# Indexer keys, head weights and low rank in one projection; the router's logits in four column groups

## The chip, the cores and the metric

The kernel runs on one core of one Trainium2 chip. The metric is the device time of one launch in microseconds, as the median of several runs.

## The reference

Two decoder layers on 256 tokens of width 1024, all in float32. Each layer has a mixer with four head groups, a cross attention to 256 memory rows, and a feed-forward part: dense SwiGLU in layer 0, and in layer 1 the top 2 of 8 experts. What the change touches:

```python
z = hn @ w_in                        # columns cut into a_q .. a_lr .. c_qi, c_ki, c_wi, d_uv
log_a = log_sigmoid(a_lr @ wa2 + ba) / TAU          # gated linear attention, a_lr: 16 wide
dots  = einsum('bqhd,bsd->bqsh', c_qi, c_ki)        # indexer: 8 heads of 32, one key of 32
score = einsum('bqsh,bqh->bqs', relu(dots), c_wi)   # c_wi: 8 head weights per token
_, sel = top_k(score, 64)                           # 64 keys for each token
...
logits = rmsnorm(h, norm_ffn[1]) @ router           # (256, 8), layer 1 only
top_v, top_i = top_k(logits, 2); gates = softmax(top_v)
```

## The kernel before

The work of each engine is one written-out instruction stream; the engines meet only in semaphores, and nothing is reordered. Activations are kept transposed (`xnT`: features on partitions, 8 tiles of 128 features by 256 tokens). A projection is either `on_features` (weights stationary, 8 matmuls of 256 tokens, result with features on partitions) or `on_tokens` (activations stationary, the weights' columns stream through, result with tokens on partitions). A float32 matmul is two MATMUL instructions in the trace, each with a weight load of its own, so 8 matmuls are `x16` there. A float32 transposition by `pe.transpose` is one.

Weights lie packed in DRAM in units. SyncE loads them in order into a ring of seven slots (`RING`, 4096 floats on each partition), and a slot is loaded anew when TensorE has used it up (`slot_free`). In the mixer the units are: U_QI (indexer queries, keys, head weights), U_A, U_AG (with the low-rank columns), U_CQ, U_CV, U_BU, U_UV.

The mixer of a layer on TensorE begins so: the rows of `h` are turned and normed; queries `qi` (16 matmuls); keys `ki` (8, 32 wide); head weights by `on_tokens` (16 matmuls that stream 8 columns each, L1593); in layer 0 a small bias matmul and three `keep_busy` matmuls (products that nobody reads, L1560), in layer 1 the first half of `a`; then `dots(1)` (L1658). ScalarE copies the keys to four places (L728), scales the head weights (`wis`, L729), later takes the relu of the dots (L741). VectorE then runs `score_and_take(1)` and `(0)`: the weighted sum over heads and 8 rounds of max and replace (L1092 to L1102), and behind them it copies the low rank `lr` (L1067). In layer 0, TensorE also turns the memory rows between the dots and `a` (L1574, memT). After `a`, `av` and `dots(0)` come `lr` (8 matmuls, 16 wide), `ag`, the first half of `q`, the matmul `logit` that needs VectorE's copy of `lr` (L1713), the rest of `q`, `k`, `cv`, and then `att` (L1729), which waits for results of ScalarE and VectorE that follow from `logit`.

The router in layer 1: TensorE turns the rows of `h` by plain matmuls with the identity (L1990), VectorE and ScalarE scale them into `xnT`, two feature tiles each in turn (L1355, L865), 8 matmuls of 8 columns give the logits (L1997), ScalarE copies them (L868), two transpositions put tokens on partitions, and VectorE chooses the experts (from L1365) and builds the tables of jobs. A first expert job of 64 tokens then starts on nine weight units that are loaded ahead: seven in the ring and two in `extra`. The second of these is loaded when `rlog_ps` is 1. The jobs that follow are 21 units each, 2 MB a unit.

Of the kernel before, what the change touches and what calls it, by code (L numbers as in the profile page):

```python
# [8 lines left out]
P = 128  # L9
# [5 lines left out]
ACT = mybir.ActivationFunctionType  # L15
# [4 lines left out]
KT = D // P  # L20
# [44 lines left out]
def packed_blocks():  # L65

    for layer in range(DEPTH):
        for s, (lo, hi) in enumerate(IN_UNITS):
            yield ("in_units", layer, s), "w_in", layer, (0, D), (lo, hi)
        yield ("wkv", layer), "xa_wkv", layer, (0, D), (0, 2 * GW)  # L70
        for i, m in enumerate(WOUT_ORDER):
            yield ("wout", layer, i), "w_out", layer, (256 * m, 256 * m + 256), (0, D)
        yield ("wq", layer), "xa_wq", layer, (0, D), (0, GW)
        yield ("wo", layer), "xa_wo", layer, (0, GW), (0, D)
    for c, n in enumerate(FFN_TILES):
        f0 = P * sum(FFN_TILES[:c])
        for w, name in enumerate(("ffn_w1", "ffn_w3")):
            yield ("ffn", 3 * c + w), name, 0, (0, D), (f0, f0 + n * P)
        yield ("ffn", 3 * c + 2), "ffn_w2", 0, (f0, f0 + n * P), (0, D)
# [7 lines left out]

def pack_weights(inputs):

    return np.concatenate([rows_on_partitions(inputs[name][index, r0:r1, c0:c1])  # L90
                           for _, name, index, (r0, r1), (c0, c1) in packed_blocks()])
# [79 lines left out]
IN_UNITS = ((C_QI, C_UV), (0, 512), (C_AG, C_BU), (C_CQ, C_CV), (C_CV, C_QI), (C_BU, C_CQ), (C_UV, IN_W))  # L171
# [10 lines left out]
for _key, _, _, (_r0, _r1), (_c0, _c1) in packed_blocks():  # L182
    PACKED[_key] = (_at, _at + (_r1 - _r0) * (_c1 - _c0))
    _at = PACKED[_key][1]
# [4 lines left out]

CONST = {}  # L190
_at = 0
for _name, _w in (("ident", P), ("vis", 256), ("reset", 256), ("bd", 256), ("tril", P), ("inv", 512),
                  ("before", P), ("ones", P), ("iota", P), ("eidx", 8), ("erev", 8), ("limit", 16)):
# [5 lines left out]
def shape_constants():  # L199
# [21 lines left out]
    put("erev", 8 - np.arange(8)[None, :])  # L221
    put("limit", np.concatenate(([SMALL], np.full(N_EXP - 1, SMALL - 1), [SMALL + P], np.full(N_EXP - 1, P)))[None, :])
# [14 lines left out]
def build(nc, A, out):  # L237
    ctx = ExitStack()
    with ctx:
# [76 lines left out]
        wa2 = sb("wa2", [GLA_RANK, P])  # L316
# [44 lines left out]
        def count(layer, no, each, off):  # L361
# [12 lines left out]
        lrT = qidx[0:GLA_RANK, 768:1024]  # L374
# [24 lines left out]
        lgT = wsT[0:N_EXP, 0:2, :].rearrange("p a b -> p (a b)")  # L399
# [20 lines left out]
            sel_ready rank_ps jobs_ready j_now j_s j_a j_tps j_th j_t j_yps j_yv j_ya j_g j_gps j_gtps j_gh j_gl  # L420
# [11 lines left out]
        g_ps = {n: slot_free[ENDS[n][0]] if n in ENDS else sem(f"ps_{n}") for n in GROUPS}  # L432
# [69 lines left out]
        def _(sp):  # L502
# [5 lines left out]
            for layer in range(DEPTH):  # L508
# [24 lines left out]

                for s, (lo, hi) in enumerate(IN_UNITS):
                    unit(0, s, ring[:, s, 0:KT * (hi - lo)], packed("in_units", layer, s))
                    if s == 0:
                        for i, name in enumerate(("gla_norm", "sgu_ln_g", "sgu_ln_b")):
                            sp.dma_start(bc[:, i, :], A[name][lay].broadcast_to([P, GW])).then_inc(S["loaded_par"], 16)
                        sp.dma_start(wa2[:, :], A["gla_wa2"][lay].rearrange("e r c -> (e r) c")).then_inc(S["loaded_par"], 16)
# [135 lines left out]
        def _(act):  # L675
# [20 lines left out]
            for layer in range(DEPTH):  # L696
# [171 lines left out]
            act.activation(lgT, ps[4][0:N_EXP, 0:SEQ], ACT.Copy).then_inc(S["xT_a"], 1)  # L868
# [132 lines left out]
        def _(dve):  # L1001
# [37 lines left out]
            for layer in range(DEPTH):  # L1039
# [36 lines left out]
                out_of("qi", qiT, v3(ps[4], 0, 512, 2))  # L1076
                if layer < 1:
# [3 lines left out]
                dve.wait_ge(g_ev["ki"], L1)  # L1081

# [25 lines left out]
                out_of("lr", lrT, ps[4][0:GLA_RANK, 0:256])  # L1108
# [445 lines left out]
        def _(pe):  # L1554
# [65 lines left out]
            for layer in range(DEPTH):  # L1620
# [5 lines left out]
                def w_in(u):  # L1626
                    lo, hi = IN_UNITS[u]
# [612 lines left out]
```

## Time and profile before

| | |
|---|---|
| median of 3 runs | 1389.37 us (1389.14 to 1391.38) |
| the profiled execution: time, span | 1391.46 us, 1389.7 us |
| busy PE, VectorE, ScalarE, GpSimd | 93%, 35%, 27%, 6% of the span |
| the chain that ended last | PE 62%, DMA 32%, VectorE 4%, ScalarE 1%, issue 1% |
| DMA | 433.51 MB, mean 312 GB/s; 424 to 430 GB/s in most slices of the experts' stage |

Layer 0 fills about 0 to 384 us of the span, layer 1 up to the router 384 to 557, router and choice 557 to 576, the experts' jobs 576 to 1380. The chain is followed back from the last instruction, so a piece of time that stands in it would shorten the span if it went, until the next thing comes last. PE rows give the operands' names, partitions times stationary columns, and the shape that streams.

### The profile page before, as it was taken

The page shows a single profiled execution, that of the slowest core. Times are in us where ns is not written, and L with a number is a line of the kernel's source. Part 1 is how long each engine was busy: PE and PEld are TensorE (multiplying, and loading weights), DVE is VectorE, ACT ScalarE, POOL GpSimd, SP SyncE. Part 2 cuts the span into 40 slices and gives each one's busy share as a digit, 9 for nine tenths or more (in the row PEclk, how much of TensorE's full clock was granted, in tenths as well). Part 3 has the DMA queues.
Part 4 walks back from the last instruction along what each step waited for, and adds up shares of the span by engine and source line. Part 5 has one row for each costly group of instructions (what it writes and reads, how often), then busy time and mean ns, then how long its engine had stood idle before and what let it go on. Part 6 is the DMA issues. An engine that isn't in the chain of part 4 may idle for free.

```text
span 1389.7 us, 15762 instructions
## 1 busy us (share of the span) xinstructions
PE 1286.5 (93%) x6338; PEld 785.7 (57%) x6338; DVE 484.4 (35%) x819; ACT 373.7 (27%) x574; POOL 79.9 (6%) x68
## 2 busy tenths in 40 slices
PE   7999999999999999999989879779779778999996
PEld 5777888888888688634323224224224225788532
DVE  1627267777626453600101001001001004988102
ACT  2244154444323423301101001001001005776102
POOL 0263000000004600000000000000000000000000
PEclk9999999999999999999999999999999999999998
DMA  9431633443181308799999999999999999999895
GB/s 361 177 116 37 231 133 137 177 186 137 40 352 65 117 1 365 306 417 428 427 428 426 429 428 430 428 428 427 430 429 428 429 427 430 427 428 379 365 428 244
DMA packets 37416, 433.51 MB, mean 312 GB/s; under 512 B 5726, under 2 KB 7924, under 8 KB 9588
## 3 DMA queue, kind: packets, MB, share of 16 engines
q1 hardware_dynamic: 37172, 432.25, 75.4%
q8 instruction: 37, 0.61, 0.2%
q0 software_dynamic: 192, 0.53, 0.1%
q14 instruction: 15, 0.12, 0.0%
HBM read 431.71 MB, written 1.05 MB: 311 GB/s over the span
## 4 chain that ended last, share of the span: by engine, by line
PE 62%; DMA 32%; DVE 4%; ACT 1%; issue 1%; SPq 0%; DVEq 0%; ACTq 0%
DMA ring<-in_experts 31%; PE bank L2089 10%; PE bank L2169 9%; PE bank L1588 8%; PE bank L1975 6%; PE bank L1593 5%; PE bank L2099 5%; PE bank L1611 4%; PE bank L1979 3%; PE bank L1574 1%; PE bank L1865 1%; PE bank L1866 1%; PE bank L1872 1%; PE bank L2022 1%; PE bank L2047 1%; PE bank L1560 1%
## 5 line engine op out<-in xcount | busy, mean ns | idle before, releaser
L2089 PE MATMUL bank<-ring,xs 128*64 128x512 f32 x1552 | 352.1, 597 | 41.2 <-DMA ring<-in_experts 41.2
L2089 PEld LDWEIGHTS bank<-ring,xs 128*64 128x64 f32 x1552 | 109.6, 137 | 247.9 <-issue 228.4
L2099 PE MATMUL bank<-ring,s_act 128*64 128x512 f32 x768 | 176.3, 597 | 34.5 <-DMA ring<-in_experts 34.3
L1477 DVE TENSOR_TENSOR s_act<-wsT,bank 128x256 f32<-128x256 f32 x49 | 20.6, 421 | 510.8 <-ACT wsT L903 510.8
L2099 PEld LDWEIGHTS bank<-ring,s_act 128*64 128x64 f32 x768 | 55.6, 137 | 142.8 <-issue 131.4
L1975 PE MATMUL bank<-x_both,wf_hi 128*128 128x512 f32 x336 | 118.9, 396 | 0.0
L903 ACT ACTIVATE wsT<-bank 128x256 f32<-128x256 f32 x49 | 18.8, 383 | 336.3 <-PE bank L2047 336.3
L1588 PE MATMUL bank<-xnT,ring 128*128 128x256 f32 (+2 forms) x448 | 102.5, 388 | 0.6 <-ACT bias L752 0.6
L1501 DVE TENSOR_TENSOR ring_lo<-ring,w_hi 128x2048 fp32r<-128x2048 f32 (+1 forms) x44 | 96.0, 2193 | 20.2 <-ACT w_hi L960 20.2
L838 ACT ACTIVATE wf_hi<-ring 128x1024 fp32r<-128x1024 f32 x66 | 69.8, 1060 | 98.6 <-PE bank L1975 67.5
L1979 PE MATMUL bank<-x_both,wf_lo 128*128 128x256 f32 x336 | 94.1, 280 | 0.0
L1272 DVE TENSOR_TENSOR wf_lo<-ring,wf_hi 128x1024 fp32r<-128x1024 f32 x66 | 80.5, 1223 | 33.4 <-ACT wf_hi L838 33.4
L1588 PEld LDWEIGHTS bank<-xnT,ring 128*128 128x128 f32 (+2 forms) x448 | 80.5, 182 | 18.5 <-issue 2.1
L960 ACT ACTIVATE w_hi<-ring 128x2048 fp32r<-128x2048 f32 (+1 forms) x44 | 80.7, 1839 | 34.6 <-PE bank L2169 29.8
L899 ACT ACTIVATE j_act<-bank 128x512 f32<-128x512 f32 x49 | 29.3, 597 | 191.4 <-PE bank L2089 191.4
L1593 PE MATMUL bank<-ring,xnT 128*128 128x256 f32 (+2 forms) x320 | 78.5, 400 | 0.0
L2169 PE MATMUL bank<-w_hi,xg 128*128 128x512 f32 x224 | 72.8, 402 | 2.6 <-DVE xg L1508 2.6
L1975 PEld LDWEIGHTS bank<-x_both,wf_hi 128*128 128x128 f32 x336 | 63.1, 188 | 14.9
L1593 PEld LDWEIGHTS bank<-ring,xnT 128*128 128x128 f32 x320 | 56.4, 193 | 20.9 <-issue 16.0
L1979 PEld LDWEIGHTS bank<-x_both,wf_lo 128*128 128x128 f32 x336 | 63.5, 189 | 0.9
L2169 PEld LDWEIGHTS bank<-w_hi,xg 128*128 128x128 f32 x224 | 42.9, 192 | 13.7 <-issue 3.5
L2047 PEld LDWEIGHTS bank<-cst,j_act 128*128 128x128 f32 x224 | 24.0, 141 | 40.9 <-issue 40.1
(361 smaller groups left out, 1459.8 us busy)
## 6 DMA issues: line engine op xcount, KB each, us to landing
ring<-in_experts SPq DMA_DIRECT2D x166, 2048.0 KB, 29.2
ring<-in_packed SPq DMA_DIRECT2D x18, 1536.0 KB, 6.9
ring<-in_packed SPq DMA_DIRECT2D x11, 2048.0 KB, 10.2
ring<-in_packed SPq DMA_DIRECT2D x16, 1024.0 KB, 4.9
extra<-in_experts SPq DMA_DIRECT2D x2, 2048.0 KB, 11.8
ring<-in_packed SPq DMA_DIRECT2D x2, 1184.0 KB, 6.1
ring<-in_packed SPq DMA_DIRECT2D x2, 1088.0 KB, 10.9
h<-in_x SPq DMA_DIRECT2D x2, 512.0 KB, 4.0
```

Source lines behind the costliest of these rows:

```text
L838: act.activation(as_piece(w, ffn_hi(i)), weights, ACT.Copy).then_inc(S["hi_ready"], 1)
L960: act.activation(w_hi[:, i % NB, 0:hi - lo], ring[:, slot, lo:hi], ACT.Copy)\
L1272: dve.tensor_tensor(as_piece(w, ffn_lo(i)), weights, as_piece(w, ffn_hi(i)), sub)\
L1501: dve.tensor_tensor(ring_lo[slot][:, lo:hi], ring[:, slot, lo:hi], w_hi[:, i % NB, 0:hi - lo], sub).then_inc(S["lo_ready"], 1)
L1588: i = mm(dst, w[:, k, :], src[:, k, :], start=k == 0, stop=k == KT - 1)
L1593: i = mm(dst, src[:, k, P * t:P * t + P], w[:, k, :], start=k == 0, stop=k == KT - 1)
L1611: ins = mm(dst, x, y, start=opens and n % 3 == 0, stop=closes and n % 3 == 2)
L1975: ins = mm(dst[:, :], wh[:, k, :], x_both[:, k, :], start=k == 0, stop=False, skip_group_check=True)
L1979: ins = mm(dst[:, 0:SEQ], wl[:, k, :], x_both[:, k, 0:SEQ], start=False, stop=k == KT - 1, skip_group_check=True)
L2089: i = mm(ps[d % 2][SMALL * side:SMALL * side + SMALL, :], xs[:, k, :], weights(u)[:, at:at + FC], start=k == 0, stop=k == KT - 1)
L2099: i = mm(ps[6 + half][SMALL * side:SMALL * side + SMALL, :], s_act[:, d % 4, x + side, :], weights(u)[:, at:at + FC], start=d == 0 and x = ...
L2169: ins = mm(dst[:, :], st_, mv, start=opens, stop=closes)
```

## The change

Layout of the weights: U_QI now holds queries, keys, the 16 low-rank columns at column 32 of the key group, 16 columns of zeros, and the 8 head weights at column 64. U_AG loses the low rank. One `on_features` of 72 columns replaces keys (32), head weights and low rank (16), and its rows land on partitions 0, 32 and 64. VectorE copies head weights and low rank out at once, TensorE turns the head weights by two small transpositions behind `dots(1)`, and VectorE scales them into `wis`. `ag` has a new wait for the first scoring, since it overwrites the bank. In the router the rows of `h` are turned by `pe.transpose`; the logits are four partial sums, one for each group of 32 columns of the array, two matmuls each; ScalarE copies 104 rows in place of 8, and a matmul with the constant `parts` adds the four parts and turns them.

```diff
+IN_UNITS = (((C_QI, C_WI), (C_LR, C_BU), (None, AT_WI - AT_LR - GLA_RANK), (C_WI, C_UV)),
+            ((0, 512),), ((C_AG, C_LR),), ((C_CQ, C_CV),), ((C_CV, C_QI),), ((C_BU, C_CQ),), ((C_UV, IN_W),))
...
 ScalarE
                 for q in range(4):
-                    act.activation(kiT[32 * q:32 * q + 32, :], ps[5][0:32, 0:256], ACT.Copy)
-                act.activation(wis[:, :, :], v3(ps[5], 256, 272, 2), ACT.Copy,
-                               scale=float(IDX_HEADS ** -0.5 * IDX_DIM ** -0.5)).then_inc(g_ev["ki"], 1)
+                    i = act.activation(kiT[32 * q:32 * q + 32, :], ps[5][0:32, 0:256], ACT.Copy)
+                i.then_inc(g_ev["ki"], 1)
...
-            act.activation(lgT, ps[4][0:N_EXP, 0:SEQ], ACT.Copy).then_inc(S["xT_a"], 1)
+            act.activation(lgT, ps[4][0:LG_ROWS, 0:SEQ], ACT.Copy).then_inc(S["xT_a"], 1)
...
 VectorE
                 out_of("qi", qiT, v3(ps[4], 0, 512, 2))
+                group("ki")
+                dve.tensor_copy(wiT, ps[5][AT_WI:AT_WI + IDX_HEADS, 0:256])
+                dve.tensor_copy(lrT, ps[5][AT_LR:AT_LR + GLA_RANK, 0:256]).then_inc(g_ev["lr"], 1)
+                dve.wait_ge(S["wi_ps"], L1)
+                link(dve.tensor_scalar(wis[:, :, :], v3(ps[5], 256, 272, 2), float(IDX_HEADS ** -0.5 * IDX_DIM ** -0.5), None,
+                                       mult))
...
-                out_of("lr", lrT, ps[4][0:GLA_RANK, 0:256])
                 group("logit")
...
 TensorE
-                on_features(ps[5][0:32, 0:256], w[:, :, 256:288])
-                for t in range(TT):
-                    i = on_tokens(ps[5][:, 256 + 8 * t:264 + 8 * t], w[:, :, 288:296], t)
-                i.then_inc(g_ps["ki"], 1)
+                on_features(ps[5][0:AT_WI + IDX_HEADS, 0:256], w[:, :, 256:256 + AT_WI + IDX_HEADS]).then_inc(g_ps["ki"], 1)
...
                 dots(1, 256).then_inc(S["dots_ps"], 1)
+                pe.wait_ge(g_ev["lr"], L1)
+                for t in range(TT):
+                    i = pe.transpose(ps[5][:, 256 + IDX_HEADS * t:256 + IDX_HEADS * (t + 1)], wiT[:, P * t:P * t + P],
+                                     ident[AT_WI:AT_WI + IDX_HEADS, AT_WI:AT_WI + IDX_HEADS])
+                i.then_inc(S["wi_ps"], 1)
...
                 pe.wait_ge(arrived[U_AG], landed[0])
+                pe.wait_ge(S["scored"], first)
...
-                on_features(ps[4][0:GLA_RANK, 0:256], w[:, :, 256:272]).then_inc(g_ps["lr"], 1)
...
-                    i = mm(xT(kt)[:, P * t:P * t + P], h[:, t, P * kt:P * kt + P], ident, start=True, stop=True)
+                    i = pe.transpose(xT(kt)[:, P * t:P * t + P], h[:, t, P * kt:P * kt + P], ident)
...
-            for kt in range(KT):
-                if kt % 2 == 0:
-                    b = kt // 2
+            for q in (0, 2):
+                for b in (q, q + 1):
                     normed(1, norm_no(1, 2), b)
-                i = mm(ps[4][0:N_EXP, 0:SEQ], routw[:, kt, :], xnT[:, kt, :], start=kt == 0, stop=kt == KT - 1)
+                for x in range(2):
+                    for b in (q, q + 1):
+                        i = mm(ps[4][QUADRANT * b:QUADRANT * b + N_EXP, 0:SEQ], routw[:, 2 * b + x, :], xnT[:, 2 * b + x, :],
+                               start=x == 0, stop=x == 1, tile_position=(0, QUADRANT * b))
...
-                i = pe.transpose(ps[5][:, N_EXP * t:N_EXP * t + N_EXP], lgT[:, P * t:P * t + P], ident[0:N_EXP, 0:N_EXP])
+                i = mm(ps[5][:, N_EXP * t:N_EXP * t + N_EXP], lgT[:, P * t:P * t + P], cc("parts")[0:LG_ROWS, :],
+                       start=True, stop=True)
```

TensorE, layer 0, from the projection of the queries to the first half of `ag`, before (a matmul is one row here, `bank` is any PSUM bank, `qidx` holds the indexer's queries and keys):

```order
L1588 MATMUL bank<-xnT,ring 32x256 x8
L1593 MATMUL bank<-ring,xnT 128x8 x16
L1649 MATMUL bank<-gla,kdec 4x384
L1560 MATMUL bank<-cst 128x256 x3
L1658 MATMUL bank<-qidx 128x256 x8
L1574 MATMUL bank<-diag,memT 128x128 x16
...
L1658 MATMUL bank<-qidx 128x128 x8
L1588 MATMUL bank<-xnT,ring 16x256 x8
L1593 MATMUL bank<-ring,xnT 128x256 x16
```

The same stretch of the changed kernel, whose lines have other numbers:

```order
L1610 MATMUL bank<-xnT,ring 72x256 x8
L1667 MATMUL bank<-gla,kdec 4x384
L1582 MATMUL bank<-cst 128x256 x3
L1676 MATMUL bank<-qidx 128x256 x8
L1689 MATMUL bank<-cst,qidx 128x8 x2
L1596 MATMUL bank<-diag,memT 128x128 x16
...
L1676 MATMUL bank<-qidx 128x128 x8
L1615 MATMUL bank<-ring,xnT 128x256 x16
```

The 16 matmuls of 8 columns and the 8 of 16 rows are gone, and two transpositions (L1689) stand behind the dots.

VectorE in the same place of the changed kernel (before, `qidx<-bank 128x512` is followed at once by the reciprocals for the memory rows):

```order
L1086 COPY qidx<-bank 128x512
L1097 COPY qidx<-bank 8x256
L1098 COPY qidx<-bank 16x256
L1100 TENSOR_SCALAR wis<-bank 128x16
L1033 RECIPROCAL st<-st 128x1
L1034 TENSOR_SCALAR diag<-cst,st 128x128
```

Two copies and the scaling have come ahead of the factors `diag` that TensorE's transpositions of the memory rows need.

## Rows read from the trace of the kernel before

**Rows 1.** The page: its span, and the granted clock in 40 slices.

```profile
span 1389.7 us, 15762 instructions
...
PEclk9999999999999999999999999999999999999998
```

**Rows 2.** The chain of work that ended last, layer 0: start us, us, what.

```profile
26.85 3.67 PE bank L1593 x32
31.25 2.33 PE bank L1560 x6
33.59 1.86 PE bank L1658 x16
```

**Rows 3.** The same chain, layer 1.

```profile
400.90 4.24 PE bank L1593 x32
405.13 6.34 PE bank L1588 x16
411.47 1.12 PE bank L1658 x16
```

**Rows 4.** Busy time by stretch: each engine, its instructions, granted clock, DMA share, GB/s.

```profile
31.18:35.38 4.20, 4.20 (x23) 2.68 (x23) 0.45 (x2) 4.09 (x11) 0.77 (x1) 0.59 1.02 425
403.80:410.60 6.80, 6.80 (x20) 5.71 (x21) 0.00 (x0) 1.67 (x5) 0.00 (x0) 0.50 0.96 364
```

**Rows 5.** Timeline of layer 0: start us, us, engine, line, operation, idle before.

```profile
34.23 0.29 DVE L1015 TENSOR_SCALAR diag<-cst,st 128x128 f32<-128x128 f32 x1
...
35.38 3.84 PE L1574 MATMUL bank<-diag,memT 128*128 128x128 f32 x32
...
59.53 3.61 PE L1588 MATMUL bank<-xnT,ring 128*16 128x256 f32 x16 [0.61 <-ACT bias L752]
```

**Rows 6.** Timeline of layer 1.

```profile
415.13 0.48 DVE L1092 SCALAR_TENSOR_TENSOR score<-r,wis,cst 128x256 f32<-128x256 f32 x1 [17.08 <-ACT r L741]
...
424.08 3.63 PE L1588 MATMUL bank<-xnT,ring 128*16 128x256 f32 x16
...
438.59 0.67 PE L1713 MATMUL bank<-qidx,wa 16*128 16x256 f32 x2 [0.32 <-DVE qidx L1067]
...
446.25 1.69 ACT L771 ACTIVATE r<-gla 32x256 f32<-32x256 f32 x4 [0.49 <-DVE gla L1115]
...
456.56 1.88 PE L1729 MATMUL bank<-r,gla 128*128 128x512 f32 x4
```

**Rows 7.** Timeline of the router in layer 1.

```profile
556.93 3.73 PE L1990 MATMUL bank<-cst,h 128*128 128x128 f32 x32
...
559.36 1.77 DVE L1355 TENSOR_SCALAR xnT<-bank,pcol 128x256 f32<-128x256 f32 x4 [0.94 <-PE bank L1990]
...
559.83 1.71 ACT L865 ACTIVATE xnT<-bank,pcol 128x256 f32<-128x256 f32 x4
...
560.59 3.62 PE L1997 MATMUL bank<-xnT,routw 128*8 128x256 f32 x16
...
561.43 2.48 DVE L1362 SCALAR_TENSOR_TENSOR r<-h,st,uvg 128x1024 f32<-128x1024 f32 x2
...
565.10 0.49 DVE L1365 TENSOR_SCALAR score<-bank,st 128x8 f32<-128x8 f32 x2 [1.18 <-PE bank L2002]
```

**Rows 8.** Timeline of layer 0, two halves of the array's columns.

```profile
123.96 0.43 PE L1809 MATMUL bank<-zeros,gla 128*64 128x256 f32 x1
...
123.97 0.43 PE L1809 MATMUL bank<-Sst,gla 128*64 128x256 f32 x1
...
124.23 0.38 PE L1809 MATMUL bank<-zeros,gla 128*64 128x256 f32 x1
```

**Rows 9.** Busy time of line L1913 alone: PE, its weight loads, granted clock.

```profile
178.10:180.40 2.30, 2.10 (x16) 1.66 (x16) 1.00 0.48 96
```

**Rows 10.** Timeline: SyncE's issues of expert weights.

```profile
579.86 20.42 SPq L581 DMA_DIRECT2D ring<-in_experts  x6
```

**Rows 11.** The chain again, expert stage.

```profile
683.65 23.70 DMA ring<-in_experts
```

More of the change, by code:

```diff
@@ L67, in packed_blocks @@
     for layer in range(DEPTH):
[L68 to L70 removed]
+        for s, columns in enumerate(IN_UNITS):
+            yield ("in_units", layer, s), "w_in", layer, (0, D), columns
+        yield ("wkv", layer), "xa_wkv", layer, (0, D), ((0, 2 * GW),)
         for i, m in enumerate(WOUT_ORDER):
[L72 to L74 removed]
+            yield ("wout", layer, i), "w_out", layer, (256 * m, 256 * m + 256), ((0, D),)
+        yield ("wq", layer), "xa_wq", layer, (0, D), ((0, GW),)
+        yield ("wo", layer), "xa_wo", layer, (0, GW), ((0, D),)
     for c, n in enumerate(FFN_TILES):
@@ L85, in rows_on_partitions, with columns_of @@
     return np.ascontiguousarray(block.reshape(rows // P, P, cols).swapaxes(0, 1)).reshape(-1)
+def columns_of(rows, columns):
+    return np.concatenate([np.zeros((len(rows), hi), np.float32) if lo is None else rows[:, lo:hi] for lo, hi in columns], axis=1)
 def pack_weights(inputs):
-    return np.concatenate([rows_on_partitions(inputs[name][index, r0:r1, c0:c1])
-                           for _, name, index, (r0, r1), (c0, c1) in packed_blocks()])
+    return np.concatenate([rows_on_partitions(columns_of(inputs[name][index, r0:r1], columns))
+                           for _, name, index, (r0, r1), columns in packed_blocks()])
 def pack_experts(inputs):
@@ L169, with unit_width @@
 C_CQ, C_CK, C_CV, C_QI, C_KI, C_WI, C_UV = 1040, 1296, 1552, 1808, 2064, 2096, 2104
-IN_UNITS = ((C_QI, C_UV), (0, 512), (C_AG, C_BU), (C_CQ, C_CV), (C_CV, C_QI), (C_BU, C_CQ), (C_UV, IN_W))
+QUADRANT = 32
+AT_LR, AT_WI = QUADRANT, 2 * QUADRANT
+IN_UNITS = (((C_QI, C_WI), (C_LR, C_BU), (None, AT_WI - AT_LR - GLA_RANK), (C_WI, C_UV)),
+            ((0, 512),), ((C_AG, C_LR),), ((C_CQ, C_CV),), ((C_CV, C_QI),), ((C_BU, C_CQ),), ((C_UV, IN_W),))
+def unit_width(s):
+    return sum(hi if lo is None else hi - lo for lo, hi in IN_UNITS[s])
 U_QI, U_A, U_AG, U_CQ, U_CV, U_BU, U_UV = range(7)
@@ L181 @@
 PACKED, _at = {}, 0
-for _key, _, _, (_r0, _r1), (_c0, _c1) in packed_blocks():
-    PACKED[_key] = (_at, _at + (_r1 - _r0) * (_c1 - _c0))
+for _key, _, _, (_r0, _r1), _columns in packed_blocks():
+    PACKED[_key] = (_at, _at + (_r1 - _r0) * sum(hi if lo is None else hi - lo for lo, hi in _columns))
     _at = PACKED[_key][1]
 R_MIX, R_XA, R_MEM, R_FFN, R_BA, R_PB, R_PS, R_SB, N_ROWS = 0, 8, 16, 24, 32, 33, 35, 37, 41
+LG_ROWS = 3 * QUADRANT + N_EXP
 CONST = {}
@@ L532, in unit @@
                     sp.dma_start(dst, src).then_inc(arrived[s], 16)
-                for s, (lo, hi) in enumerate(IN_UNITS):
-                    unit(0, s, ring[:, s, 0:KT * (hi - lo)], packed("in_units", layer, s))
+                for s in range(len(IN_UNITS)):
+                    unit(0, s, ring[:, s, 0:KT * unit_width(s)], packed("in_units", layer, s))
                     if s == 0:
```

24 lines of the change are left out of this document (12 added, 12 removed).

## Prediction

> **What bounds the kernel now.** I read the page first: the span, and the granted clock, nine tenths or more in every slice but the last [rows 1]. Then the chain of work that ended last. Up to the experts it is almost all TensorE, piece behind piece, and three of its pieces are what the change is about: 32 instructions of L1593, which stream 8 columns each, take 3.67 us in layer 0 and 4.24 in layer 1 [rows 2, 3]. In the experts' stage the chain turns to DMA at 683.65 [rows 11]. That does not make the time before it free: the weights are loaded into slots that TensorE must give back, and SyncE issues again only at 579.86, when the first job has used its first unit [rows 10]. From there DMA and TensorE lean on one another to the end, so whatever brings the first job forward brings the end forward by as much. The question is thus how much earlier the first job starts.
>
> The last view is the table by stretches, cut where pieces of the chain looked too long. 16 instructions of 128x256 cost 3.6 us elsewhere [rows 5, 6], but the same 16 behind the head weights of layer 1 cost 6.34 [rows 3]. The table says why: from 403.80 to 410.60 the granted clock was 0.50, the lower of the two levels, 1.2 GHz, and from 31.18 to 35.38 it was 0.59 on the mean [rows 4]. Both times TensorE had just spent about 4 us on the narrow products. They cost more than their own time.
>
> **Layer 0.** Gone are the head weights, 3.67 us. The key group has 72 columns in place of 32; what a matmul costs is what streams, 256 columns, and 8 of them with 16 stationary columns took 3.61 us [rows 5], like those with 128, so I cost the widening at nothing. Three `keep_busy` matmuls took 2.33 us and the dots 1.86 at the low clock [rows 2]; at the full clock they are 6 x 3.6/16 = 1.35 and, from layer 1, 1.12 [rows 3], a gain of 1.7. The two small transpositions cost 0.13 each, from 16 transpositions in 2.10 us [rows 9]: 0.26. TensorE would then reach the memory rows at 35.38 - 3.67 - 1.7 + 0.26 = 30.3. But `diag` of those rows comes from ScalarE and VectorE. VectorE made it at 34.23 [rows 5], and that path moves only by the 3.67, to 30.6; ahead of it now stands the scaling of the head weights, which waits for the transpositions (30.3) and takes some 0.2 us. The factor is ready at about 31.0, and the gain so far is 4.3, not 5.1. Queued behind VectorE's new wait are just these factors, and for them TensorE waits: that is the 0.8. Later the low rank goes, another 3.6 [rows 5]. The wait of 0.61 for ScalarE ahead of it stays, since both sides moved alike; it now holds `ag`. **Layer 0: 7.9 us.**
>
> **Layer 1.** Head weights 4.24 less 0.26; the low clock behind them 6.34 - 3.5 = 2.8; the low rank 3.55; and the wait of `logit` for VectorE's copy of the low rank, 0.32 [rows 6], goes too, since the copy now comes before the scoring. Sum 10.65, say **10.7 us**. What is late next? VectorE's scoring was nearly level with TensorE. It starts at 415.13, on the relu of the dots, and that moves by all but the low rank and the wait, 6.8 us. Behind it come the bias of the logits, ScalarE's exponentials, and the block-diagonal queries (L771), which end at 446.25 + 1.69 = 447.94 [rows 6], now 441.1. TensorE asks for them at 456.56, now 445.9. The slack shrinks from 8.6 to 4.8 and holds. The new wait of `ag` for the first scoring asks for eight sums of about 0.5 us from 408.3 on, done at 412.5, when TensorE comes there at 417: free. If that cover went, each us would be paid in full.
>
> The added DMA traffic is 32 columns more in one unit and 16 less in another, of 1024 rows of 4 bytes: 131 KB, 0.3 us at 425 GB/s [rows 4], ahead of units that are in place long before their use. The change moves no issue of SyncE past another, and the slots of the key unit and of `ag` come free earlier. ScalarE loses one small copy. I cost these at nothing.
>
> **The router.** 32 instructions in 3.57 us (556.93 to 560.6) become 16 transpositions, 2.1 us at the rate of [rows 9]. This gives little: VectorE's scaling starts 0.5 earlier, but ScalarE's starts at 559.83, held by its own sums of squares, and ends at 561.54 [rows 7]. The logits now begin when ScalarE has its first pair, about 560.7, and their second half when it has the last, 561.6. What follows depends on whether column groups work side by side. The trace has halves of the array doing so: two matmuls with 64 columns each start at 123.96 and 123.97, the next pass at 124.23 [rows 8], 0.27 for two where one behind the other would be 0.44. At that rate the last four matmuls are four pairs of instructions, 1.1 us, and end at 562.7; before, 16 in a row ended at 564.1. That is 1.4 less. The wider copy and the summing matmul (two passes and full weights in place of one each) give back about 0.1. VectorE must be free as well: its two products (L1362) take 2.48 us and end near 563.4, and the choice would start at 563.8 against 565.10 [rows 7]. **Router: 1.3 us**; none if the groups run one behind the other (8 x 0.22 = 1.8 from 561.6 or the full 3.5 from 560.7 both end near 564), and 1.6 if the groups cost less than the halves. I take 1.3, since the row of the halves is the same kind of packing.
>
> Here a rule of the skill speaks against the change. The router's turning was made of plain matmuls, and 16 transpositions take their place. In this trace 16 such transpositions ran in 2.10 us at a granted clock of 1.00 [rows 9], so I take no loss of clock. The Trainium skill, "TensorE: Matmul & The Clock Gate", Part 4 on PE-mode transpose, says that transpositions do not count as activity for the clock as matmuls do; by that rule the low clock would come in the router. That is the first rival below.
>
> **The sum.** 7.9 + 10.7 + 1.3 = 19.9 us. Against the profiled execution that is 1391.46 - 19.9 = 1371.6. The median of the runs shown is 2.1 lower, 1389.37, and gives 1369.5. Some of the difference may lie in the two low-clock stretches that I price at 4.5 us together, which need not be as long in each execution; so I say 1370.0.
>
> **Rivals.**
> - The clock falls at a new place (0.19). In the router TensorE now transposes, waits about 1 us for ScalarE, does short bursts and waits again. For it: both falls of before followed thin work. Against: it did not fall at 178. Priced by the rows, a stretch at 0.5 costs half its length: 4.2 us at 0.59 cost 1.7, 6.8 us cost 2.8 [rows 4]. In the router it would take away the 1.3 and delay the products of rank or gather by 2 or so: 1373.5. The same happens if it falls when TensorE waits for the memory rows' copies in layer 0.
> - Something hides the gain (0.08). The slack of 4.8 us in layer 1 is my own working, and POOL's scaling and SyncE's loads follow the same scoring. If another chain takes over behind `att` in both layers and only half of the mixers' 18.6 is kept: 1379. Against: the chain shows TensorE nearly without a break up to the router.
> - The column groups do nothing (0.10): the router gives 0, 1371.3. Within the range.
> - Slower than before (0.03): the low clock, once it falls in the router, stays. In the experts' stage TensorE is on the chain alone until 683.65 [rows 11]; each us at 1.2 GHz there costs half. The gain of 20 is used up after 40 us of it, and 60 us would give 1370 + 30 = 1400. Against it: the two stretches of before ended within 7 us, as soon as full matmuls streamed.
> - As forecast: 0.60.
>
> **How the numbers follow.** The likeliest case alone spans 1368 to 1372.5: the router's 0 to 1.6, and 1.5 us either way for how long the low clock lasted in the runs shown. The clock rival adds up to 1376; below, 1366.5 takes in a median that keeps the whole price of the low clock and 1.6 in the router with 2 us of scatter as in the three runs. 1366.5 to 1376 leaves out the hidden gain and the slower case, 0.11, and with the tails of the others 0.18. A measurement of this kernel tells a change from none at about 0.2%, 2.8 us. Faster by more than that: 0.95, all cases but the last and a gain lost nearly whole; within it 0.02; slower 0.03.
>
> **What the profile after would show.** No instructions of 128x8 in the mixers; granted clock 1.00 in both places; the first half of `a` in layer 1 in 3.5 us; `dots(1)` some 6.5 us after the keys; the first scoring at about 408.3 - 7.9 = 400; `att` reached without a wait; 16 logit instructions starting in pairs 0.27 apart, the choice 1.3 us earlier against the turning's start; SyncE's issue of 579.86 at about 560. The prediction is wrong if the clock row is below 1.00 in the router, if TensorE waits ahead of `ag` or `att`, or if SyncE's issue moves by less than 17.

## The result and the profile after

The changed kernel takes 1371.14 us (median of 4 runs, 1370.39 to 1372.91), the kernel before on the same chip 1390.38 us (4 runs, 1389.14 to 1393.55). The ratio is 0.9863, with a 95% interval from 0.9844 to 0.9881: 19.2 us faster, where 20 was forecast (1370.0, range 1366.5 to 1376.0). The profiled execution took 1372.91, with a span of 1369.3.

From the page of the changed kernel, its span and the granted clock in 40 slices:

```profile
span 1369.3 us, 15555 instructions
...
PEclk9999999999999999999999999999999999999998
```

The chain of work that ended last, changed kernel (start us, us, what), which answers to [rows 2, 3, 11]: layer 0, layer 1, experts.

```profile
28.10 1.49 PE bank L1582 x6
29.59 1.08 PE bank L1676 x16
31.62 3.82 PE bank L1596 x32
...
84.42 1.72 PE bank L1752 x4
...
397.04 1.08 PE bank L1676 x16
398.77 3.46 PE bank L1610 x16
...
664.14 23.55 DMA ring<-in_experts
```

`att` of layer 0 in the same chain of the kernel before:

```profile
91.79 1.72 PE bank L1729 x4
```

The narrow matmuls of the head weights have gone. The three `keep_busy` take 1.49 in place of 2.33, the dots 1.08 in place of 1.86, and the first half of `a` in layer 1 takes 3.46 in place of 6.34. The DMA transfer at which the chain turns starts 19.51 us earlier (683.65 to 664.14).

Busy time by stretch, changed kernel, the places of [rows 4] and the router (stretch, length, busy us of PE, its weight loads, VectorE, ScalarE, POOL, then the granted clock, DMA share, GB/s):

```profile
26.50:31.60 5.10, 4.23 (x30) 2.44 (x29) 1.47 (x5) 4.11 (x9) 0.77 (x1) 1.00 1.00 419
31.60:38.70 7.10, 5.57 (x42) 5.20 (x43) 3.58 (x10) 3.69 (x11) 2.13 (x3) 1.00 1.03 431
393.50:398.60 5.10, 5.10 (x39) 4.26 (x38) 1.01 (x3) 1.91 (x5) 0.00 (x0) 1.00 1.04 442
...
542.60:544.40 1.80, 1.72 (x17) 0.70 (x17) 1.77 (x3) 0.67 (x2) 0.00 (x0) 1.00 1.00 419
```

The clock is 1.00 in each of them. Neither low stretch of [rows 4] is left, and none came in the router, behind the 16 transpositions.

The timeline of the changed kernel (start us, us, engine, line, operation, idle time before it and who ended it), at the first projection and at the places of [rows 5 to 7] and [rows 10]:

```profile
16.84 10.53 PE L1610 MATMUL bank<-xnT,ring 128*128 128x256 f32 x48
...
30.77 0.17 DVE L1100 TENSOR_SCALAR wis<-bank 128x16 f32<-128x16 f32 x1 [2.52 <-PE bank L1689]
...
31.18 0.29 DVE L1034 TENSOR_SCALAR diag<-cst,st 128x128 f32<-128x128 f32 x1
...
31.62 3.81 PE L1596 MATMUL bank<-diag,memT 128*128 128x128 f32 x32 [0.89 <-DVE diag L1034]
...
55.73 7.14 PE L1615 MATMUL bank<-ring,xnT 128*128 128x256 f32 x32 [0.61 <-ACT bias L771]
...
400.28 0.48 DVE L1115 SCALAR_TENSOR_TENSOR score<-r,wis,cst 128x256 f32<-128x256 f32 x1 [1.88 <-ACT r L760]
...
404.48 0.06 DVE L1120 MEMSET st<- 128x1 f32 x1
...
409.72 7.17 PE L1615 MATMUL bank<-ring,xnT 128*128 128x256 f32 x32
...
430.10 1.69 ACT L790 ACTIVATE r<-gla 32x256 f32<-32x256 f32 x4 [0.49 <-DVE gla L1137]
...
438.27 1.88 PE L1752 MATMUL bank<-r,gla 128*128 128x512 f32 x4
...
538.81 1.03 PE L2013 MATMUL bank<-cst,h 128*128 128x128 f32 x8
...
542.68 1.77 PE L2021 MATMUL bank<-xnT,routw 128*8 128x256 f32 x16 [1.23 <-ACT xnT L884]
542.79 2.48 DVE L1384 SCALAR_TENSOR_TENSOR r<-h,st,uvg 128x1024 f32<-128x1024 f32 x2
...
545.58 0.49 DVE L1387 TENSOR_SCALAR score<-bank,st 128x8 f32<-128x8 f32 x2 [0.30 <-PE bank L2027]
...
560.33 3.76 SPq L601 DMA_DIRECT2D ring<-in_experts  x2
```

The first projection of the kernel before:

```profile
16.17 10.68 PE L1588 MATMUL bank<-xnT,ring 128*128 128x256 f32 x48
```

Read it as a ladder. In layer 0 TensorE waits 0.89 for `diag`, which stands behind the scaling of the head weights. `ag` starts in layer 0 at 55.73, with the wait of 0.61 that the low rank had before. In layer 1 the first scoring starts at 400.28, against 415.13 [rows 6]. L1120 is its end, at 404.5, and `ag` comes there at 409.72. The block-diagonal queries end at 430.10 + 1.69 = 431.8, and `att` (L1752) asks for them at 438.27, against 456.56 [rows 6], that is 18.3 earlier. The router's turning starts 18.1 earlier (556.93 to 538.81), the choice of experts 19.5 (565.10 to 545.58), SyncE's issue 19.5 (579.86 to 560.33). The span is 20.4 shorter; what came on top behind the issue, 0.9, lies in the experts' stage, and I did not trace it to an operation.

### The profile page after: what moved, and what is told of

It reads as the page before. It is cut to its first block, busy times and chain, and to the rows that moved or that the text cites. A ratio compares the mean times of both kernels' runs of the same rounds, so it can differ in the third digit from the quotient of the medians.

```text
span 1369.3 us, 15555 instructions
## 1 busy us (share of the span) xinstructions
PE 1263.6 (92%) x6232; PEld 770.6 (56%) x6232; DVE 486.1 (36%) x823; ACT 373.4 (27%) x572; POOL 80.4 (6%) x68
## 4 chain that ended last, share of the span: by engine, by line
PE 63%; DMA 32%; DVE 2%; ACT 1%; issue 1%; SPq 0%; DVEq 0%; ACTq 0%
DMA ring<-in_experts 32%; PE bank L2115 10%; PE bank L2195 9%; PE bank L1610 8%; PE bank L1998 6%; PE bank L1615 6%; PE bank L2125 5%; PE bank L1633 4%; PE bank L2002 3%; PE bank L1596 2%; PE bank L1888 1%; PE bank L1895 1%; PE bank L1889 1%; PE bank L2048 1%; PE bank L2073 1%; PE bank L1582 1%
## 5 line engine op out<-in xcount | busy, mean ns | idle before, releaser
L1610 PE MATMUL bank<-xnT,ring 128*128 128x256 f32 (+1 forms) x416 | 92.0, 380 | 0.0
L1610 PEld LDWEIGHTS bank<-xnT,ring 128*128 128x128 f32 (+1 forms) x416 | 76.7, 186 | 12.3 <-issue 0.7
L1615 PE MATMUL bank<-ring,xnT 128*128 128x256 f32 (+1 forms) x256 | 70.4, 433 | 0.6 <-ACT bias L771 0.6
L1615 PEld LDWEIGHTS bank<-ring,xnT 128*128 128x128 f32 x256 | 48.5, 190 | 20.2 <-issue 15.1
```

The lines of the kernel that those rows point to most:

```text
L1610: i = mm(dst, w[:, k, :], src[:, k, :], start=k == 0, stop=k == KT - 1)
L1615: i = mm(dst, src[:, k, P * t:P * t + P], w[:, k, :], start=k == 0, stop=k == KT - 1)
```

## The experiments

Each is an edit of the changed kernel unless it says otherwise. "Added" in the text is against the 1371.14 of the changed kernel; ratios are against the kernel before, run beside it on the same chip. The median of the kernel before lay between 1390.38 and 1393.19 in these groups of runs, so a difference of medians across groups is uncertain by 2 to 3 us, and small ones are read from the traces.

### The two halves of the change

**Router alone**, on the kernel before (the copy of `lgT`, the transpositions of `h`, the grouped logits and the matmul with `parts`), and **mixers alone**, the changed kernel with these lines undone.

> The kernel before with the router's part of the change alone: rows of h turned by transpositions, logits in four column groups, the four parts summed by a matmul. My sum: 1.3 to 1.5 us less than before, within the scatter of the runs, so the trace must tell it: from the start of the turning to VectorE's choice 8.2 us became 6.8 in the changed kernel, and here the same 6.8. Rival, that the router's gain in the changed kernel is an effect of when the mixers end: 8.2 us here.

> The changed kernel with the router as before. If the two mixers carry the gain: 18 us less than before, ratio 0.987, and 1.4 us above the changed kernel. Rival, that some of the gain needs both parts (the first expert job, the order of the loads): under 15 us less than before.

Router alone: 1388.52 us (7 runs, 1388.03 to 1391.7), before 1393.19 (10 runs); ratio 0.9971 (0.9957 to 0.9985). Mixers alone: 1370.75 us (4 runs, 1370.38 to 1373.47), the same before; ratio 0.9839 (0.9823 to 0.9856). Taken as they stand, 4.7 and 22.4 us add up to more than the 19.2 of the whole change, and the interval of router alone (2.1 to 6.0 us) does not hold 1.3. In these runs the kernel before was 2.8 us above its median beside the changed kernel, which goes into both differences; its clock was lower (below). Mixers alone misses its expectation for the same reason: 22.4 for the 18 expected, and 0.4 below the changed kernel where 1.4 above was expected. Medians don't separate 1.4 us here, so I read the traces: from the start of the turning to the choice it takes 562.79 - 556.03 = 6.76 us with the router's part and 547.00 - 538.83 = 8.17 without, against 6.77 and 8.17 in the changed kernel and the kernel before. The router's part gives 1.40 us in both surroundings, and the rest is the mixers'.

The router-alone kernel still has the narrow products in both layers. Its busy time by stretch, the first in layer 0, the second from the narrow products of layer 1 on:

```profile
29.78:36.60 6.82, 6.82 (x25) 4.50 (x28) 0.45 (x2) 4.25 (x11) 0.77 (x1) 0.50 1.01 422
403.20:410.40 7.20, 7.20 (x53) 6.51 (x52) 0.00 (x0) 1.67 (x5) 0.00 (x0) 1.00 1.04 430
```

In layer 0 the clock was at 0.50 for 6.8 us, where before had 4.2 us at 0.59 [rows 4]. In layer 1 it did not fall at all, behind the same 32 instructions. So whether a low stretch follows the narrow products depends on the execution: the mixers' code is the same in both kernels.

### What goes before the low clock

Four kernels put other work behind the key group of both layers, and leave everything else of the change in place.

```diff
...
 narrow_back: 16 matmuls, 128 stationary columns, 8 streamed
+                for t in range(TT):
+                    i = on_tokens(ps[5][:, 256 + 8 * t:264 + 8 * t], w[:, :, 256 + AT_WI:256 + AT_WI + IDX_HEADS], t)
...
 wide_instead: 8 matmuls, 128 stationary columns, 256 streamed
+                for _ in range(8):
+                    i = mm(ps[5][:, 256:512], ident, cc("vis"), start=True, stop=True)
...
 thin_long: 16 matmuls, 8 stationary columns, 256 streamed
+                for _ in range(2):
+                    i = on_features(ps[5][0:8, 256:512], w[:, :, 0:8])
...
 turning_long: 56 transpositions, 128x128
+                for n in range(56):
+                    i = pe.transpose(ps[5][:, 256 + P * (n % 2):384 + P * (n % 2)], h[:, 0, P * (n % 8):P * (n % 8) + P], ident)
```

> The changed kernel with the 16 matmuls that stream 8 columns put back behind the 72-column group in both layers; their product is overwritten and the low rank stays merged. It adds work only. Theory, that they cost their own time and then the low clock: granted clock 0.5 in two stretches again, 3.4 to 6.8 us each, and 4.5 us more in layer 0 and 7 in layer 1, 11 to 12 us above the changed kernel. Rival, that the clock falls for another reason (the place, the low rank): 3.7 to 4 us a layer, 7.5 to 8 in all, and a clock of 1.00.

> The changed kernel with 8 matmuls of 256 columns in the place of the narrow ones, into a bank's half that is overwritten; they take 3.5 us a layer, nearly what the narrow ones took. It adds work only. Theory of the clock: it stays at 1.00, and the time is 7 us above the changed kernel, 4 to 5 below the kernel with the narrow ones back. Rival: the same time as with the narrow ones within 1 us, since both only delay what follows.

> The changed kernel with 16 matmuls added behind the key group in both layers that stream 256 columns each, as the wide ones did, but have only 8 stationary columns; 6.9 us a layer, result overwritten. It adds work only. If the clock looks at how densely columns stream, it stays at 1.00 up to the router and the time is 13.8 us above the changed kernel, 1385. If it looks at the stationary columns too (the keys of 32 and the low rank of 16 columns would then be part of the fall that the kernel before shows), it falls in both layers and the time is 3 to 7 us more, 1388 to 1392.

> The changed kernel with 56 transpositions of 128x128 added in the same place, 0.13 us each by the row of 16 in 2.10 us, 7.3 us a layer, overwritten. It adds work only. My reading of the rows (16 such at a clock of 1.00): no fall, 14.6 us above the changed kernel, 1386. The Trainium skill's rule that transpositions don't count for the clock: a fall in both layers, 3 to 7 us more.

Medians, 4 runs each: `narrow_back` 1379.26 (ratio 0.9901, 0.9883 to 0.9919), `wide_instead` 1377.59 (0.9891, 0.9874 to 0.9908), `thin_long` 1385.66 (0.9952, 0.9935 to 0.9969), `turning_long` 1382.68 (0.9936, 0.9916 to 0.9955). Added: 8.1, 6.5, 14.5 and 11.5.

`narrow_back` by stretch: the narrow products of layer 0, what follows them, the same in layer 1.

```profile
26.43:29.90 3.47, 3.47 (x34) 3.45 (x33) 0.00 (x0) 0.00 (x0) 0.00 (x0) 1.00 0.97 411
31.73:38.56 6.83, 5.95 (x35) 4.86 (x34) 0.98 (x5) 4.85 (x11) 0.77 (x1) 0.50 1.03 433
398.85:402.32 3.47, 3.47 (x34) 3.47 (x33) 0.00 (x0) 0.00 (x0) 0.00 (x0) 1.00 1.06 446
402.32:409.00 6.68, 6.68 (x47) 5.66 (x47) 1.01 (x3) 3.47 (x9) 0.00 (x0) 1.00 1.00 419
```

`turning_long` by stretch, the transpositions of layer 0 and of layer 1:

```profile
27.19:33.60 6.41, 6.41 (x58) 5.96 (x56) 0.26 (x1) 0.26 (x1) 0.00 (x0) 1.00 0.98 413
399.40:405.50 6.10, 6.10 (x58) 6.10 (x57) 0.00 (x0) 0.00 (x0) 0.00 (x0) 1.00 1.03 438
```

The narrow products cost their own time in each layer (3.5 us) and a low stretch behind them in layer 0 of this execution, none in layer 1. So `narrow_back` came out at 8.1, below the 11 to 12 expected with two stretches, and only 1.7 above the same time of wide work, where 4 to 5 was expected. The profiles are sharper than the medians. The first projection of layer 0 starts anywhere from 15.57 to 17.47 us in the fourteen of them; counted from there to `att` of layer 1, the changed kernel takes 421.4 us, `narrow_back` 9.8 more, `wide_instead` 6.9, `thin_long` 14.2, `turning_long` 12.2. Of the 9.8, 6.2 come ahead of `a` in layer 0, so the one low stretch cost 2.7 beside its 3.5 of work; the rest, 3.6, is the work in layer 1. The other three are added work alone. `wide_instead` (6.5, two times 3.5 expected), `thin_long` (7.0 us of work in each layer, 14.5) and `turning_long` (56 in about 6.1 us, 11.5) cost about their own time, at a granted clock of 1.00 in both layers of all three; `thin_long` shows it as `turning_long` does:

```profile
27.00:34.00 7.00, 7.00 (x34) 2.95 (x33) 0.00 (x0) 0.00 (x0) 0.00 (x0) 1.00 0.99 417
400.00:408.00 8.00, 8.00 (x38) 3.33 (x36) 0.00 (x0) 0.00 (x0) 0.00 (x0) 1.00 0.95 402
```

Expected of `turning_long` was 0.13 us a transposition; in a long row it is 6.10/56 = 0.109.

So of four kinds of work that fill TensorE's time, only the one that streams few columns was followed by the lower level, 1.2 GHz. It did not come behind few stationary columns (`thin_long`), nor behind transpositions. All fourteen profiles say the same: three kernels have the narrow products in both layers (before, router alone, `narrow_back`), and the clock fell at four of these six places; of the 22 such places in the other eleven kernels it fell at one, in the wait that `late_scoring_b` makes (below).

The narrow products may not be the whole of it. Over all runs with a clock on record, the mean granted clock was 0.990 to 0.995 in the kernel before (28 runs), 0.993 to 0.996 in `narrow_back` (4), 0.995 to 0.997 in the changed kernel (4). Put back behind the key group of 72 columns, the same products went with less low clock than they had before. What else in the kernel before goes with the fall, no run tests.

The Trainium skill, "TensorE: Matmul & The Clock Gate", Part 4 on PE-mode transpose, says that transpositions don't count as activity in the way matmuls do; 6.1 us of them, twice, did not bring the clock down here, so in this kernel the measurement decides against it. They stood behind full-rate matmuls; whether transpositions could bring the clock up from the lower level, no run tests.

### How near the new wait of `ag` is

The scoring of layer 1 is made later by additions on VectorE whose result is not used, 11 of them (5 us) or 20 (9 us):

```diff
+                if layer:
+                    dve.wait_ge(S["rel"], first)
+                    for _ in range(11):
+                        link(dve.tensor_tensor(score[:, 0, :], cc("vis"), cc("reset"), add))
                 score_and_take(1, 256)
```

> The changed kernel with 11 additions on VectorE, 0.45 us each, 5 us in all, ahead of the scoring of layer 1. It adds work only. In the changed kernel the block-diagonal queries are ready at 431.8 and TensorE asks for them at 438.3, 6.5 us of slack: nothing changes, the product att starts within 0.2 us of where it did. Rival, that ScalarE or GpSimd behind the scoring are as late as VectorE: up to 5 us.

> The same with 20 additions, 9 us. The slack of 6.5 us is used up and TensorE waits ahead of att, 2.5 us later against the start of the layer. Rival: nothing, if the slack is larger than the rows show, or all of 9 us, if the scoring is what TensorE follows.

With 11: 1371.26 us (one run). With 20: 1378.92 (one run). The timeline of the kernel with 11, end of the first scoring and start of `ag`:

```profile
409.37 0.06 DVE L1120 MEMSET st<- 128x1 f32 x1
...
409.56 7.17 PE L1619 MATMUL bank<-ring,xnT 128*128 128x256 f32 x32
```

The same of the kernel with 20, and `att`:

```profile
413.95 0.06 DVE L1120 MEMSET st<- 128x1 f32 x1
...
414.11 9.67 PE L1619 MATMUL bank<-ring,xnT 128*128 128x256 f32 x32 [4.04 <-issue]
...
445.15 1.88 PE L1756 MATMUL bank<-r,gla 128*128 128x512 f32 x4
```

And by stretch, with 20:

```profile
405.00:412.40 7.40, 5.07 (x37) 4.08 (x35) 6.84 (x17) 0.60 (x1) 0.00 (x0) 1.00 0.26 85
412.40:419.20 6.80, 5.09 (x12) 4.10 (x13) 6.34 (x20) 2.49 (x5) 0.00 (x0) 0.50 0.19 76
```

With 11, the scoring ends at 409.4 and `ag` starts at 409.56 without a wait: 5 us of slack, used up and free. `att` starts at 438.12, within the 0.2 us expected of 438.27. With 20, TensorE stands 4.04 us ahead of `ag`; the profile puts it down to "issue", but it ends 0.1 us behind L1120, whose semaphore it asks for. The clock fell to 0.50 in this wait, and `ag` took 9.67 in place of 7.17. `att` starts 445.15 - 438.27 = 6.9 later, and the time is 7.8 more (one run). Both kinds of loss are there, 6.5 us in all: the wait, and 2.5 us by the clock behind it. The remaining 1.3 I did not trace. I had expected 2.5 us, at `att`; the wait of `ag` is the nearer one.

### The router's two parts

`no_groups` keeps the turning by transpositions and computes the logits in 8 full passes, as before; `plain_turning` keeps the groups and turns by plain matmuls.

```diff
 no_groups
+            for kt in range(KT):
+                if kt % 2 == 0:
+                    b = kt // 2
+                    normed(1, norm_no(1, 2), b)
+                i = mm(ps[4][0:N_EXP, 0:SEQ], routw[:, kt, :], xnT[:, kt, :], start=kt == 0, stop=kt == KT - 1)
...
 plain_turning
-                    i = pe.transpose(xT(kt)[:, P * t:P * t + P], h[:, t, P * kt:P * kt + P], ident)
+                    i = mm(xT(kt)[:, P * t:P * t + P], h[:, t, P * kt:P * kt + P], ident, start=True, stop=True)
```

> The changed kernel with the logits as before, eight matmuls in a row into 8 rows and two transpositions of them, while the rows of h are still turned by transpositions. If the column groups carry the router's gain: the choice comes 8.1 to 8.3 us after the turning starts, as before, against 6.8 in the changed kernel; the logits start at ScalarE's first pair and end 3.5 us later. Rival, that the earlier scaling carries it: 7 us.

> The changed kernel with the rows of h turned by plain matmuls again, column groups kept. ScalarE's scaling starts after its own sums of squares in both, so the last logits wait for the same thing: 6.8 us from the turning's start to the choice as in the changed kernel, at most 0.4 more. Rival, that the transpositions carry the gain: 7.5 or more.

Times of one run each: 1371.66 and 1371.8, too near the changed kernel to tell anything. The traces can. `no_groups`:

```profile
538.86 1.03 PE L2013 MATMUL bank<-cst,h 128*128 128x128 f32 x8
...
541.80 3.62 PE L2020 MATMUL bank<-xnT,routw 128*8 128x256 f32 x16 [0.32 <-DVE xnT L1377]
...
546.31 0.49 DVE L1387 TENSOR_SCALAR score<-bank,st 128x8 f32<-128x8 f32 x2 [1.00 <-PE bank L2025]
```

`plain_turning`:

```profile
538.97 3.73 PE L2013 MATMUL bank<-cst,h 128*128 128x128 f32 x32
...
542.83 1.92 PE L2021 MATMUL bank<-xnT,routw 128*8 128x256 f32 x16
...
543.47 2.48 DVE L1384 SCALAR_TENSOR_TENSOR r<-h,st,uvg 128x1024 f32<-128x1024 f32 x2
...
545.89 0.49 DVE L1387 TENSOR_SCALAR score<-bank,st 128x8 f32<-128x8 f32 x2
```

From the turning's start to the choice: 8.17 us before, 7.45 with the transpositions alone, 6.92 with the groups alone, 6.77 with both. The transpositions alone give 0.72, where I had expected 0.1 at most. What I had missed is the start of the logits in feature order. In the kernel before it waits for TensorE's own turning (560.59 [rows 7]); here they begin with VectorE's pair, which transpositions make ready earlier, at 541.80, and need ScalarE's pair only two passes later. The groups alone give 1.25: 16 instructions in 1.92 us in place of 3.62. The choice then follows directly on VectorE's two products (543.47 + 2.48 = 545.95), so VectorE is the bound there, and the transpositions add only 0.15 by letting it start earlier. The two parts overlap; 0.72 and 1.25 do not add up.

### A version that undoes the wait for `diag`

The wait of 0.89 ahead of the memory rows came with the change. `early_factors` makes the factors of layer 0 ahead of the key group's copies; the second kernel, `early_less_busy`, also drops the second `keep_busy(6, 3)`, which stands on TensorE's path behind the memory rows.

```diff
 VectorE (ScalarE's root_mean of the memory rows moves likewise ahead of its group("ki"))
+                if layer < 1:
+                    factors(layer, 2)
                 group("ki")
...
-                link(dve.tensor_scalar(wis[:, :, :], v3(ps[5], 256, 272, 2), float(IDX_HEADS ** -0.5 * IDX_DIM ** -0.5), None,
-                                       mult))
+                dve.tensor_scalar(wis[:, :, :], v3(ps[5], 256, 272, 2), float(IDX_HEADS ** -0.5 * IDX_DIM ** -0.5), None,
+                                  mult).then_inc(S["wi_v"], 1)
+                dve.wait_ge(S["wi_v"], L1)
                 if layer < 1:
-                    factors(layer, 2)
...
 TensorE, in the memory rows' loop
+                        if isinstance(no, int) and t == 0 and kt == 2:
+                            pe.wait_ge(S["wi_v"], 1)
...
 early_less_busy alone
-                    keep_busy(6, 3)
```

> The changed kernel, with ScalarE's sums of squares of the memory rows and VectorE's factors of layer 0 ahead of the copies of the key group, in time in which both wait. TensorE stood 0.89 us ahead of the memory rows for VectorE's factor; it then starts them behind the small transpositions, and layer 0 is 0.8 to 0.9 us shorter, the time 1370.3. Rival: nothing, if TensorE then waits for the bias row or for the copy of the head weights.

> The same, and without the three matmuls of 256 columns that nobody reads behind the memory rows in layer 0, 1.3 us. If the clock holds through the 1.5 us of waiting that stand ahead of them: 2.2 us less than the changed kernel in all, 1369. If it falls there, the first projection behind it runs in part at 1.2 GHz, as in the kernel before in layer 1, and costs 1.7 to 3.4 us more: 1371 to 1373 and a clock row below 1.00 between 36 and 45 us.

`early_factors`: 1370.03 us (5 runs, 1368.82 to 1371.84), before 1391.61 (11 runs); ratio 0.9845 (0.9831 to 0.9858). `early_less_busy`: 1369.33 us (5 runs, 1366.55 to 1370.11), same before; ratio 0.9841 (0.9829 to 0.9854). The timeline of `early_factors`, dots, memory rows, `a`:

```profile
28.84 1.15 PE L1680 MATMUL bank<-qidx 32*128 32x256 f32 x16
...
29.98 3.84 PE L1600 MATMUL bank<-diag,memT 128*128 128x128 f32 x32
...
37.23 1.03 PE L1614 MATMUL bank<-xnT,ring 128*128 128x256 f32 x4
```

`early_less_busy`, the same three:

```profile
28.29 1.15 PE L1680 MATMUL bank<-qidx 32*128 32x256 f32 x16
...
29.43 3.84 PE L1600 MATMUL bank<-diag,memT 128*128 128x128 f32 x32
...
35.35 1.03 PE L1614 MATMUL bank<-xnT,ring 128*128 128x256 f32 x4
```

From the dots to `a` is 8.39 us in the first and 7.06 in the second, against 9.25 in the changed kernel: 0.86 and 2.2 less, as expected, with the clock at 1.00 in both. Both gains are still there at `att` of layer 1 (0.84 and 2.17 less, counted from the first projection). The medians follow in sign and about in size (1.1 and 1.8 below 1371.14), but these kernels ran in another group, and a gain of 1 to 2 us against the changed kernel is shown by the traces, not by the intervals, which overlap.

### The scatter of the times

For each run the mean granted clock is on record. From one group of runs, the kernel before (the two fastest and the two slowest of ten) and the changed kernel with the router undone (all four):

```
kernel before    1390.24 us at 0.994   1390.39 at 0.995   ...   1394.92 at 0.991   1395.51 at 0.990
mixers alone     1370.38 us at 0.997   1370.73 at 0.997   1370.76 at 0.996   1373.47 at 0.996
```

The kernel before goes from 1390.4 at 0.995 to 1395.5 at 0.990: in these ten runs time and clock go together. An estimate from the rows: a stretch at 0.50 that lasts L us costs L/2 where TensorE is busy and lowers the mean clock by 0.5 L/1390, so 0.001 of mean clock is 2.8 us of low clock, or 1.4 us of time; 0.005 would be 7 us, and 5.1 are measured. The clock is not the whole scatter. In seven other runs of the kernel before (1390.1 to 1392.9 us, 0.992 to 0.994) time and clock show no common order; the first projection starts up to 1.9 us apart in the profiles; and the slowest run above has 3.4 us around its span where the other nine have 1.8 to 2.1. The kernel before and the changed kernel had 0.992 and 0.996 in their profiled executions, and 0.004 is 5.6 us, give or take 1.4 for the rounding, where I had priced 4.5 for the two stretches. Part of the rest stands under another name: in layer 1 the clock was low from 403.80, while the narrow products ran until 405.13: 1.3 us, half of it lost, against the 0.6 by which they took longer there than in layer 0 (4.24 against 3.67).

## Why the prediction was right, step by step

- **Layer 0, 7.9 forecast.** `att` of layer 0 starts at 84.42, against 91.79 before, and the first projection 0.67 later than before (16.84 against 16.17), which the change does not explain: 7.37 + 0.67 = 8.0 us. The wait for `diag` (0.89, forecast 0.8), the low clock ahead of it and the unchanged wait of 0.61 came as written. That the head weights' scaling is what holds it was forecast, and `early_factors` shows it: with the order undone, 0.86 comes back.
- **Layer 1, 10.7 forecast.** The projections start 7.18 earlier and `att` 18.29 earlier: 11.1. Narrow products, low clock and low rank went as priced. This is a statement on these two executions. Of the 2.8 for the low clock in layer 1 the runs show that it is not paid in each: neither router alone nor `narrow_back` had it in layer 1 of its profile. The removal of the narrow products takes away an occasion for it, and not a fixed sum. The sum leaned on both stretches of one profile; the mean clock of 0.990 to 0.995 in 28 runs bears out that the kernel before usually loses about as much.
- **Router, 1.3 forecast.** 1.40. The groups work side by side: 16 instructions took 1.77 us from first to last, where 16 in 8 full passes took 3.6. That is 0.22 us a pair or less, against the 0.27 that was priced. One bound beside the sum was miscounted, without effect: 1.8 us from 561.6 end at 563.4, not near 564; only the other bound, 3.5 from 560.7, does. VectorE's idle time ahead of the choice has shrunk from 1.18 [rows 7] to 0.30, so little is left there for a still faster TensorE. One statement was wrong: that the transpositions give little. It was true with the groups in place (0.15) but not without them (0.72). My sum kept it out, since the groups take the logits' start away from VectorE's pair.
- **What is late next.** The prediction's places in layer 1 still carry layer 0's 7.9; with that taken off, the scoring was to be done at 412.5 - 7.9 = 404.6 and TensorE at `ag` at 409.1. The profile has 404.5 and 409.7, a slack of 5.2 for 4.5. Ahead of `att`, TensorE was to ask at 438.0 for queries that are ready at 433.2; it asks at 438.3, and they are ready at 431.8, 1.4 sooner, a slack of 6.5 for 4.8. In both, `ag` is the nearer wait. (`dots(1)` start 3.3 us behind the end of the keys' matmuls and about 7 behind their start; the 6.5 among the signs fits neither.) In the expectation of `late_scoring_b` I still placed the loss at `att`, against my own two numbers, and that step fell.
- **From the router on.** SyncE's issue was forecast at about 560 and came at 560.33. All that TensorE won ahead of the experts arrived at the end: 19.5 at the choice, 19.5 at the DMA transfer where the chain turns, 20.4 at the span.
- **The median.** The sum of 19.9 was made against the profiled execution. Its span shrank by 20.4, but what lies around the span grew from 1.8 to 3.6 us (1372.91 - 1369.3); the other three runs have 1.8, 1.8 and 2.2 there. The medians differ by 19.2, and 1371.14 is 1.1 above the 1370.0 forecast. Part of the closeness is luck. From the first projection to the choice of experts the profile gained 20.2, to which the experts' stage added 0.9 that was not forecast, and the first projection came 0.67 late, also not forecast; and the medians scatter by as much.
- **The rivals.** The clock did not fall at a new place: 1.00 in the router and in the memory rows' wait. The mechanism of that rival is real, though, as `late_scoring_b` shows: a wait of 4 us brought 0.50 for 6.8 us. Nothing hid the gain. The groups did not run one behind the other. The clock did not stay low. What the prediction said against that last rival was misread, though: the low stretches of before did not end as soon as full matmuls streamed. In layer 1 these streamed from 405.13 [rows 3], and the clock was low to 410.60 [rows 4].

**What stays open.** Why the narrow products of the kernel before were followed by a low clock in both layers of its profile, and in one layer only in `narrow_back` and router alone. The experiments show what the fall came behind (few streamed columns, waiting) and what it did not come behind (few stationary columns, transpositions, wide matmuls), in one profiled execution each; not what decides it in a given execution. Waits have the same open end. In the experts' stage TensorE waits 2.6 us for VectorE once; behind it the changed kernel is at 0.50 from 1149 to 1152 us and the kernel before from 1169 to 1171, so this fall is no part of the difference, while `early_less_busy` has the same wait of 2.60 at 1144 and stays at 1.00. The Trainium skill, "TensorE: Matmul & The Clock Gate", Part 1, says of the start of a kernel that the same kernel runs 6, 11 or 14 matmuls at the lower clock, by the run. It speaks of the rise, and these falls lie in the middle of the kernel; that they too vary from execution to execution is what the profiles here show.

## What to carry to other kernels

When TensorE is the chain, look at the granted clock just behind narrow products and waits: here matmuls that stream 8 columns cost their own time and then, at four places of six, a stretch at half clock, which the profile books on the lines that follow, and which comes in some executions and not in others. Fold such products into a group whose streamed operand is already wide, and pay for it with a small transposition; then look for what the other engines now have ahead of work that TensorE waits for. Before trusting a slack, make the suspected work later by the slack and by twice as much: the first run shows that it is free, the second which wait comes first.

## What the runs showed of the hardware that I had not expected

- 56 transpositions of 128x128 in float32 took 6.1 us back to back, 0.109 each, against 0.13 in a row of 16 [rows 9], and left the clock at 1.00.
- 7 us of matmuls with 8 stationary columns, 256 streamed, kept a clock of 1.00 in both layers, as 3.5 us with 128 stationary columns did.
- Two column groups of 8 columns each run side by side in float32, as the halves of [rows 8] do: 16 instructions in 1.77 us, where 8 full passes took 3.62.
- A wait of 4 us of TensorE cost 2.5 us more, behind it, by the clock.
- The same code had a low stretch in one profiled execution and none in another: layer 1 of the kernel before (0.50 for 6.8 us) and of router alone (1.00).
